# A hybrid decoder layer on one core: the head reordered so that x and the first weights are split first

## The chip, the cores and the metric

The kernel runs on one core of one Trainium2 chip. The metric is device time in microseconds (us), from the start to the end of one execution. Lower is better.

## The reference

One layer is computed for 520 tokens: 512 of a prompt and 8 of a sample group. Only its first part matters here.

```python
xn = rmsnorm(x, g1)               # x * rsqrt(mean(x*x) + EPS) * g1
z = xn @ w_in                     # q, k, v, o, ig, fg, u, vb, ga, gb
ig = ig + b_ig
lf = log_sigmoid(fg + b_fg)
h = mlstm_branch(q, k, v, ig, lf, ...)
u = gelu(u)
vn = rmsnorm(gelu(vb), g_v)
y_b = spatial_gate(u, vn, w_s, b_s) @ w_b
```

Behind it come the branch projections, an output projection, a second norm and a causal ConvFFN with D_FF 2816. All is in float32.

## The kernel before, in words

Tensors lie feature-major: 128 features on the partitions, 520 tokens in the row, and 1024 features are eight pieces (KT). Float32 products are made from two float32r halves. A value is split into `hi`, its rounded copy (ScalarE, function `split` for weights), and `lo`, the rest (VectorE, function `low`). One output tile of 128 features takes a weight slot of 128x1024 and 48 matmuls of 260 columns: for each of the eight pieces hi\*hi, hi\*lo and lo\*hi, over two halves of the tokens (function `tile`, L1293). Slots are numbered: 0 is the gate tile (gate rows ig and fg), 1 to 8 are the eight tiles of the v branch (vb 0 to 7), 9 to 12 the q tiles, and so on through some 150 slots. Raw weights, `whi`, `wlo` and the PSUM banks `out` are each double-buffered by the slot's parity. The counter `done` rises by one with each finished tile, and slot n is split only when the tile of slot n-2 is done.

A row norm commutes with a matmul. So the gate tile and vb 0 and 1 are computed on x times its gain without the norm (`xuh`, `xul`), and their results are multiplied by the norm's factor `rbc1` afterwards. The other vb tiles and all later ones use the normed `xh`, `xl`, which cost a product on GpSimd (L1170, in place in x), a copy on ScalarE and a subtraction on VectorE (L784) for each piece.

The head, on each engine, in the written order:

- Sync issues the x chunks 0, 1 and 3 (each two pieces of x), then the weights of slots 0 and 1; ScalarE issues gains, x chunk 2 and the gate bias.
- ScalarE squares the even pieces of x, VectorE the odd ones, into two buffers `sq`. TensorE sums each square over the partitions by a matmul with ones into `aux` (32 float32 matmul instructions), and a buffer is written again only when TensorE has read it. Between the squares both engines split x; the weights of slot 0 are split before the last pair of pieces.
- ScalarE takes the root, VectorE the reciprocal (L775), and GpSimd then scales x, eight products.
- The v branch's result goes through a gelu on ScalarE into `ftmp`, is transposed on TensorE (L1322, in the middle of the next tile), copied to `g_tok` on VectorE (L842), and squared and summed on GpSimd (L1183, L1185). For vb 0 and 1 VectorE first scales the result (L789); for vb 2 to 7 gelu reads PSUM itself and so empties the bank.
- Between them VectorE does three blocks of small work on the gate rows: `gate_cumsums` (L803 to L811), `gate_maxima` (L816 to L823) and `gate_outputs` (L828 to L836), behind vb 3, 4 and 5. ScalarE makes the softplus (absolute value, exp, log, each with a table load) around vb 2 and 3.

Every engine runs its own list in order, so what stands ahead in a list is what delays the next item. Nothing behind the q tiles is touched by the change.

Of the kernel before, what the change touches and what calls it, by code (L numbers as in the profile page):

```python
# [75 lines left out]
def hybrid_layer(nc, ins, outs):  # L76
    with ExitStack() as ctx:
# [332 lines left out]
        def _(act):  # L410
# [67 lines left out]
            split(At(2))  # L478
            for k in range(4):
                normed_hi(k)  # L480
            split(At(3))
            for k in range(4, 6):
                normed_hi(k)
            scaled_vb(0)
            for k in range(6, KT):
                normed_hi(k)
            split(At(4))
            scaled_vb(1)


            def vb_step(i, t):
                n = At(S_VB + t, i, 2)
                split(n.plus(2))
                apart()
                ready(n)
                act.wait_ge(tr_done, n(-2))
                A(gvs[:, i * 2 + t, :], smp(n), ACT.Gelu_apprx_tanh)
                A(both(ftmp[t][:, :]), out2(n), ACT.Gelu_apprx_tanh).then_inc(evac[n.c % 2], 1)


            vb_step(1, 0)
            evacuated(act, At(S_GATE))
            act.wait_ge(s_const, 16)
            A(lfe[:, :], fg[:, :], ACT.Abs, bias=gb[:, 1:2])
            act.drain()
            A(lfe[:, :], lfe[:, :], ACT.Exp, scale=-1.0)
            vb_step(1, 1)
            act.drain()
            A(lfe[:, :], lfe[:, :], ACT.Ln, bias=ones[0:NH, 0:1]).then_inc(s_ln, 1)
            with act.Fori(2, 4) as i:  # L510
                for t in range(2):
                    vb_step(i, t)
# [222 lines left out]
        def _(dve):  # L735
# [26 lines left out]
            for r in range(KT // 2):  # L762
                dve.wait_ge(s_x[r], 16)
                if r >= 1:
                    dve.wait_ge(s_ssk, 2 * r)
                TT(sq[1][:, :], x0[:, 2 * r + 1, :], x0[:, 2 * r + 1, :], ALU.mult).then_inc(s_sq[1], 1)
                if r == KT // 2 - 1:
                    low(At(0))
                for k in (2 * r, 2 * r + 1):
                    dve.wait_ge(s_xuh, k + 1)  # L770
                    STT(xul[:, k, :], x0[:, k, :], gains[:, 0, k:k + 1], xuh[:, k, :].bitcast(F32),
                        ALU.mult, ALU.subtract).then_inc(s_xu, 1)
            low(At(1))
# [3 lines left out]
            ready(At(S_GATE))  # L777
            for at0, rows_ in ((0, ig), (32, fg)):
                o = TT(both(rows_[:, :]), out_ps[0][at0:at0 + NH, :, 0:HALF], both(rbc1[at0:at0 + NH, :]), ALU.mult)
            o.then_inc(evac[0], 1)  # L780
# [63 lines left out]
            def vb_step(j):  # L844

                n = At(S_VB + j)
                vb_side(j - 1)
                if 4 <= j <= 6:
                    (gate_cumsums, gate_maxima, gate_outputs)[j - 4]()
# [711 lines left out]
```

## Time and profile before

| | us |
|---|---|
| median of 3 runs | 933.81 (933.24 to 934.28) |
| the profiled execution | 933.54 |
| its span, first to last instruction | 931.2 |
| TensorE busy in matmuls | 907.6 (97%) |
| VectorE busy | 524.5 (56%) |
| ScalarE busy | 365.8 (39%) |
| GpSimd busy | 135.4 (15%) |

The profiled execution is 0.27 us below the median, and 2.3 us of it lie outside the span. TensorE is busy for 97% of the span, so the time is the sum of its work and of the few stretches in which it waits. These are at the two ends. The reader should go by where TensorE first starts real tiles, and by each gap in its row after that.

### The profile page before, as it was taken

Reading aid. Unit: us, or ns where it says so; the run is one execution under the profiler, and the core shown is the slowest. Engines: PE = TensorE matmul, PEld = TensorE weight load, DVE = VectorE, ACT = ScalarE, POOL = GpSimd, SP = SyncE. Lnnn points to the kernel's source line nnn. Section 1 sums busy time; section 2 is a strip of 40 time slices with the busy share of each in tenths; the row PEclk is TensorE's granted clock in tenths of the full one; section 3 lists DMA queues with packets and bytes.
Section 4 is the critical chain, followed back from the end, with each engine's and each line's share of the span. In section 5 each row is a group of like instructions: output and inputs, shape, how many; then the busy total and the mean of one; then the engine's idle time right before and its main releaser. Section 6 shows DMA issues by size and latency. Waiting matters only on the chain.

```text
span 931.2 us, 19618 instructions
## 1 busy us (share of the span) xinstructions
PE 907.6 (97%) x7424; PEld 899.8 (97%) x7424; DVE 524.5 (56%) x801; ACT 365.8 (39%) x550; POOL 135.4 (15%) x182
## 2 busy tenths in 40 slices
PE   7999999999999999999999999999999999999993
PEld 6999999999999999999999999999999999999993
DVE  7874555552784444433335777777777777332334
ACT  5663333543873223322223344444444444222230
POOL 1843000002451111000006600000000000000002
PEclk9999999999999999999999999999999999999997
DMA  5414233224782221342234222222222223323222
GB/s 183 124 66 151 92 113 128 79 70 161 256 287 91 89 68 68 117 156 90 90 106 103 90 91 90 90 90 90 90 90 92 91 92 99 97 83 103 83 62 92
DMA packets 30184, 100.16 MB, mean 108 GB/s; under 512 B 4524, under 2 KB 6604, under 8 KB 29896
## 3 DMA queue, kind: packets, MB, share of 16 engines
q1 hardware_dynamic: 28528, 93.46, 30.4%
q0 software_dynamic: 1328, 5.72, 2.3%
q8 instruction: 21, 0.34, 0.2%
q10 hardware_dynamic: 296, 0.55, 0.2%
q14 instruction: 11, 0.09, 0.0%
HBM read 92.37 MB, written 7.35 MB: 107 GB/s over the span
## 4 chain that ended last, share of the span: by engine, by line
PE 89%; DVE 4%; POOLq 3%; issue 2%; DMA 1%; POOL 0%; DVEq 0%; ACT 0%; ACTq 0%
PE out L1293 83%; PE aux L1293 2%; PE trp L1293 2%; POOLq L1270 2%; DVE xl L784 1%; POOLq L1268 1%; PE trp L1322 1%; DVE wlo L742 1%; DVE y L1154 1%; DMA gains<-in_gains 0%; PE aux L1427 0%; DVE ftmp L1150 0%; DMA cwb<-in_conv_wb 0%; DVE mmax L820 0%; POOL out_conv_old L1254 0%
## 5 line engine op out<-in xcount | busy, mean ns | idle before, releaser
L742 DVE TENSOR_TENSOR wlo<-raw,whi 128x1024 fp32r<-128x1024 f32 (+1 forms) x149 | 189.7, 1273 | 227.3 <-ACT whi L412 227.0
L412 ACT ACTIVATE whi<-raw 128x1024 fp32r<-128x1024 f32 (+1 forms) x149 | 156.3, 1049 | 266.0 <-PE out L1293 264.3
L1293 PE MATMUL out<-xh,whi 128*128 128x260 f32 x864 | 178.7, 288 | 1.2 <-DVE wlo L742 1.2
L1293 PE MATMUL out<-xh,wlo 128*128 128x260 f32 x864 | 173.9, 283 | 0.0
L1293 PE MATMUL out<-xl,whi 128*128 128x260 f32 x864 | 173.7, 282 | 0.0
L1293 PE MATMUL out<-x2h,wlo 128*128 128x260 f32 x704 | 141.9, 283 | 0.0
L1293 PE MATMUL out<-x2h,whi 128*128 128x260 f32 x704 | 141.8, 282 | 0.0
L1293 PE MATMUL out<-x2l,whi 128*128 128x260 f32 x704 | 141.6, 283 | 0.0
L1293 PEld LDWEIGHTS out<-xh,whi 128*128 128x128 f32 x864 | 133.4, 189 | 1.9 <-DVE wlo L742 1.4
L1293 PEld LDWEIGHTS out<-xh,wlo 128*128 128x128 f32 x864 | 133.1, 188 | 0.0
L1293 PEld LDWEIGHTS out<-xl,whi 128*128 128x128 f32 x864 | 133.0, 188 | 0.0
L1293 PEld LDWEIGHTS out<-x2h,whi 128*128 128x128 f32 x704 | 108.6, 188 | 0.1
L1293 PEld LDWEIGHTS out<-x2h,wlo 128*128 128x128 f32 x704 | 108.5, 188 | 0.0
L1293 PEld LDWEIGHTS out<-x2l,whi 128*128 128x128 f32 x704 | 108.2, 188 | 0.0
L1293 PE MATMUL out<-acth,wlo 128*128 128x260 f32 x352 | 71.0, 283 | 0.0
L1293 PE MATMUL out<-acth,whi 128*128 128x260 f32 x352 | 70.8, 282 | 0.0
L1293 PE MATMUL out<-actl,whi 128*128 128x260 f32 x352 | 70.8, 283 | 0.0
L1097 DVE TENSOR_TENSOR up<-out,rbc 128x520 f32<-128x520 f32 x44 | 30.9, 702 | 42.3 <-PE out L1293 42.2
L1293 PEld LDWEIGHTS out<-acth,wlo 128*128 128x128 f32 x352 | 54.3, 188 | 0.0
L1293 PEld LDWEIGHTS out<-acth,whi 128*128 128x128 f32 x352 | 54.2, 188 | 0.0
L1293 PEld LDWEIGHTS out<-actl,whi 128*128 128x128 f32 x352 | 54.1, 188 | 0.0
L1276 POOL COPY nconv<-up 128x10 f32 x44 | 9.0, 204 | 242.8 <-DVEq L1098 242.8
(254 smaller groups left out, 1269.5 us busy)
## 6 DMA issues: line engine op xcount, KB each, us to landing
raw<-in_w_slots SPq DMA_DIRECT2D x125, 512.0 KB, 3.3
raw<-in_w_dn SPq DMA_DIRECT2D x16, 448.0 KB, 3.3
c_ring<-in_C_state SPq DMA_DIRECT2D x8, 512.0 KB, 4.9
row<-scratch SPq DMA_DIRECT2D x8, 512.0 KB, 5.6
out_C_sample<-c_ring SPq DMA_DIRECT2D x8, 512.0 KB, 3.8
raw<-in_w_dn SPq DMA_DIRECT2D x8, 512.0 KB, 3.5
xres<-in_x_all POOLq DMA_DIRECT2D x1, 2080.0 KB, 11.2
x<-in_x_all SPq DMA_DIRECT2D x3, 520.0 KB, 5.7
```

The costliest lines, as they stand in the source:

```text
L412: return act.activation(out, in_, func, **kw_)
L742: TT(wlo[p][:, 0:width], raw[p][:, 0:width], whi[p][:, 0:width].bitcast(F32), ALU.subtract)\
L784: STT(xl[:, k, :], x0[:, k, :], gains[:, 0, k:k + 1], xh[:, k, :].bitcast(F32), ALU.mult, ALU.subtract).then_inc(s_xn, 1)
L1097: TT(both(up[t][:, 2:2 + TOK]), out2(n), both(rbc2[:, :]), ALU.mult).then_inc(evac[n.c % 2], 1)
L1154: TT(y[:, j, h], xg[:, j, h], rbcf[:, h], ALU.mult).then_inc(s_y, 1)
L1268: pool.drain()
L1270: pool.drain()
L1276: pool.tensor_copy(nconv[:, i * 2 + t, :], up[t][:, SEQ:2 + TOK]).then_inc(s_nc, 1)
L1293: return pe.matmul(*a, **k)
L1322: m = pe.transpose(trp[b.c % 2][:, c, :], ftmp[b.c % 2][:, c * P:(c + 1) * P], ident[:, :])
```

## The change

It does five things.

1. x and the first weights come first. Sync issues x chunk 0, weights 0, x chunk 3, weights 1; ScalarE issues gains, x chunks 1 and 2. ScalarE splits x piece 0, then the gate weights, then the other pieces, then the weights of slot 1; VectorE follows in the same order. No square stands between.
2. The squares move behind, all eight on ScalarE into `xsq`. VectorE adds them into `xsum` (seven additions), and one sum product on TensorE (two matmuls, four instructions) stands in the middle of vb 1, behind its first piece.
3. The gate tile's raw result is copied by ScalarE out of PSUM into `graw`, and VectorE scales it from there after vb 0 and 1.
4. All eight vb tiles use `xuh`, `xul`. So each result is first scaled by VectorE (function `scaled_vb`), which also empties the bank, and gelu (function `vb_gelu`) follows on ScalarE in `ftmp`. The normed x is first read by the q tiles; its pieces are made by ScalarE and VectorE in steps 2 to 6 (`XN_AT`).
5. The gate blocks stand one step later than before (behind vb 4, 5 and 6 by name), and the softplus stands in one piece in ScalarE's step 3.

```diff
+XN_AT = ((), (), (0,), (1, 2), (3, 4), (5, 6), (7,), ())
...
             wp = ins["w_slots"]
-            for k in (0, 1, 3):
+            for n, k in ((0, 0), (1, 3)):
                 sp.dma_start(x0[:, 2 * k:2 * k + 2, :], ins["x_all"][:, 2 * k:2 * k + 2, :]).then_inc(s_x[k], 16)
-            for n in range(2):
                 load(At(n), wp[n])
...
             act.dma_start(gains[:, :, :], ins["gains"]).then_inc(s_g, 16)
-            act.dma_start(x0[:, 4:6, :], ins["x_all"][:, 4:6, :]).then_inc(s_x[2], 16)
+            for k in (1, 2):
+                act.dma_start(x0[:, 2 * k:2 * k + 2, :], ins["x_all"][:, 2 * k:2 * k + 2, :]).then_inc(s_x[k], 16)
             act.dma_start(gb[:, :], ins["gate_b"]).then_inc(s_const, 16)
...
-                if k % 2 == 0:
-                    if k >= 2:
-                        act.wait_ge(s_ssk, k - 1)
-                    A(sq[0][:, :], x0[:, k, :], ACT.Square).then_inc(s_sq[0], 1)
-                if k == KT - 2:
-                    split(At(0))
                 A(xuh[:, k, :], x0[:, k, :], scale=gains[:, 0, k:k + 1]).then_inc(s_xuh, 1)
-            split(At(1))
-            act.wait_ge(done, 1)
+                if k == 0:
+                    split(At(S_GATE))
+            split(At(S_VB))
+
+            for k in range(KT):
+                if k == 4:
+                    split(At(S_VB + 1))
+                A(xsq[:, k, :], x0[:, k, :], ACT.Square).then_inc(s_sq, 1)
+            ready(At(S_GATE))
+            A(graw[:, :].rearrange("p (a b) -> p a b", a=2), out_ps[0][0:32 + NH, :, 0:HALF]).then_inc(evac[0], 1)
+            split(At(S_VB + 2))
+            act.wait_ge(s_ss1, 1)
...
+            def vb_gelu(j):
+
+                evacuated(act, At(S_VB + j))
+                A(gvs[:, j, :], ftmp[j % 2][:, SEQ:TOK], ACT.Gelu_apprx_tanh)
                 act.drain()
-                A(ftmp[j][:, :], ftmp[j][:, :], ACT.Gelu_apprx_tanh).then_inc(evac[(S_VB + j) % 2], 1)
...
+            for j in range(2, 8):
+
+                split(At(S_VB + j + 1))
+                if j == 2:
+                    vb_gelu(0)
+                vb_gelu(j - 1)
+                for k in XN_AT[j]:
+                    normed_hi(k)
+                if j == 3:
+                    act.wait_ge(s_gr, 1)
+                    act.wait_ge(s_const, 16)
+                    A(lfe[:, :], fg[:, :], ACT.Abs, bias=gb[:, 1:2])
+                    act.drain()
+                    A(lfe[:, :], lfe[:, :], ACT.Exp, scale=-1.0)
+                    act.drain()
+                    A(lfe[:, :], lfe[:, :], ACT.Ln, bias=ones[0:NH, 0:1]).then_inc(s_ln, 1)
+            split(At(S_VB + 9))
+            vb_gelu(7)
...
+            for k in range(KT):
+                dve.wait_ge(s_xuh, k + 1)
+                STT(xul[:, k, :], x0[:, k, :], gains[:, 0, k:k + 1], xuh[:, k, :].bitcast(F32),
+                    ALU.mult, ALU.subtract).then_inc(s_xu, 1)
+                if k == 0:
+                    low(At(S_GATE))
+            low(At(S_VB))
+            dve.wait_ge(s_sq, 2)
+            TT(xsum[:, :], xsq[:, 0, :], xsq[:, 1, :], ALU.add)
+            for k in range(2, KT):
+                if k == 5:
+                    low(At(S_VB + 1))
+                dve.wait_ge(s_sq, k + 1)
+                dve.drain()
+                m = TT(xsum[:, :], xsum[:, :], xsq[:, k, :], ALU.add)
+            m.then_inc(s_sum, 1)
+            low(At(S_VB + 2))
...
             def scaled_vb(j):
-                ready(At(S_VB + j))
-                TT(both(ftmp[j][:, :]), out2(At(S_VB + j)), both(rbc1[:, :]), ALU.mult).then_inc(s_raw, 1)
-
-            low(At(2))
-            for k in range(4):
-                normed_low(k)
+                n = At(S_VB + j)
+                ready(n)
+                if j >= 2:
+                    dve.wait_ge(tr_done, B_VB + j - 1)
+                TT(both(ftmp[j % 2][:, :]), out2(n), both(rbc1[:, :]), ALU.mult).then_inc(evac[n.c % 2], 1)
+
             scaled_vb(0)
-            low(At(3))
-            for k in range(4, KT):
-                normed_low(k)
             scaled_vb(1)
+            for at0, rows_ in ((0, ig), (32, fg)):
+                o = TT(rows_[:, :], graw[at0:at0 + NH, :], rbc1[at0:at0 + NH, :], ALU.mult)
+            o.then_inc(s_gr, 1)
 
...
-            for j in range(1, 8):
+                if j >= 3:
+                    scaled_vb(j - 1)
+                low(At(S_VB + j + 1))
+                if j == 3:
+                    vb_side(1)
+                for k in XN_AT[j]:
+                    normed_low(k)
+                if j >= 5:
+                    (gate_cumsums, gate_maxima, gate_outputs)[j - 5]()
+                vb_side(j - 1 if j >= 3 else 0)
+
+            for j in range(2, 8):
                 vb_step(j)
+            scaled_vb(7)
+            low(At(S_VB + 9))
             vb_side(7)
 
-            evacuated(dve, At(S_VB + 7))
+            dve.wait_ge(s_vbg, KT)
             TT(ssq[:, :, :], gvs[:, :, :], gvs[:, :, :], ALU.mult)
             dve.drain()
...
+            def transposes(b, evn, vb=None):
+
+                if vb is None:
+                    evacuated(pe, evn)
+                else:
+                    pe.wait_ge(s_vbg, vb + 1)
                 pe.wait_ge(tre[b.c % 2], b.half(1))
                 for c in range(NC):
...
+            def square_sums():
+
+                pe.wait_ge(s_sum, 1)
                 for a in range(2):
-                    m = MM(aux[:, a, 0:HALF], ones[:, :], sq[k % 2][:, a * HALF:(a + 1) * HALF],
-                           start=k == 0, stop=k == KT - 1)
...
+            def vb_transposes(j):
+
+                transposes(At(B_VB + j), None, vb=j)
 
             tile(At(S_GATE), xuh, xul, each=s_xu)
             tile(At(S_VB), xuh, xul)
+            tile(At(S_VB + 1), xuh, xul, mid_at=0, mid=square_sums)
             pe.wait_ge(s_tri, 1)
...
+            tile(At(S_VB + 2), xuh, xul, mid_at=4, mid=lambda: vb_transposes(0), end=lambda: vb_transposes(1))
+            for j in range(3, 8):
+                tile(At(S_VB + j), xuh, xul, mid_at=5, mid=lambda: vb_transposes(j - 1))
...
-            tile(At(S_Q), xh, xl, mid_at=5, mid=lambda: transposes(At(B_VB + 7), At(S_VB + 7)))
+            tile(At(S_Q), xh, xl, each=s_xn, mid_at=5, mid=lambda: vb_transposes(7))
```

ScalarE at the head of the program, before. `sq` are squares, `xuh` the high halves of x times gain, `whi` the high halves of weights, `rbc` the norm's factor.

```order
L412 ACTIVATE sq_119<-x_87 128x520
L412 ACTIVATE xuh<-x_87,gains 128x520 x2
L412 ACTIVATE sq_119<-x_87 128x520
L412 ACTIVATE xuh<-x_87,gains 128x520 x2
L412 ACTIVATE sq_119<-x_87 128x520
L412 ACTIVATE xuh<-x_87,gains 128x520 x2
L412 ACTIVATE sq_119<-x_87 128x520
L412 ACTIVATE whi_107<-raw_105 128x1024
L412 ACTIVATE xuh<-x_87,gains 128x520 x2
L412 ACTIVATE whi_108<-raw_106 128x1024
L412 ACTIVATE rbc_57<-aux,eps 128x520
```

The same place now:

```order
L417 ACTIVATE xuh<-x_89,gains 128x520
L417 ACTIVATE whi_110<-raw_108 128x1024
L417 ACTIVATE xuh<-x_89,gains 128x520 x7
L417 ACTIVATE whi_111<-raw_109 128x1024
L417 ACTIVATE xsq<-x_89 128x520 x4
L417 ACTIVATE whi_110<-raw_108 128x1024
L417 ACTIVATE xsq<-x_89 128x520 x4
L417 ACTIVATE graw<-out 36x520
L417 ACTIVATE whi_111<-raw_109 128x1024
L417 ACTIVATE rbc_59<-aux,eps 128x520
L417 ACTIVATE whi_110<-raw_108 128x1024
```

The squares (`xsq`) stood between the pieces of x and ahead of the gate weights; now the gate weights stand second, and the squares behind the weights of slot 1, four ahead of the weights of slot 2 and four behind.

VectorE in the middle of the v branch, before, from the split weights of slot 6 (`wlo`) to the next copy. `ig`, `lf` and `bcum` are the first gate block.

```order
L742 TENSOR_TENSOR wlo_109<-raw_105,whi_107 128x1024
L842 COPY g_tok<-trp 128x4x128
L803 TENSOR_SCALAR ig<-ig,gb 4x520
L805 TENSOR_SCALAR lf<-fg,gb 4x520
L807 TENSOR_TENSOR lf<-lf,lfe 4x520
L811 SCALAR_TENSOR_TENSOR bcum<-ones,lf 4x128 x4
L742 TENSOR_TENSOR wlo_110<-raw_106,whi_108 128x1024
L842 COPY g_tok<-trp 128x4x128
```

The same gate block now:

```order
L784 TENSOR_TENSOR ftmp_117<-out,rbc_59 128x520
L733 TENSOR_TENSOR wlo_113<-raw_109,whi_111 128x1024
L776 SCALAR_TENSOR_TENSOR xl<-x_89,gains,xh 128x520 x2
L795 TENSOR_SCALAR ig<-ig,gb 4x520
L797 TENSOR_SCALAR lf<-fg,gb 4x520
L799 TENSOR_TENSOR lf<-lf,lfe 4x520
L803 SCALAR_TENSOR_TENSOR bcum<-ones,lf 4x128 x4
L834 COPY g_tok<-trp 128x4x128
L784 TENSOR_TENSOR ftmp_118<-out,rbc_59 128x520
L733 TENSOR_TENSOR wlo_112<-raw_108,whi_110 128x1024
```

Before, gelu on ScalarE read PSUM and asked nothing of VectorE. Now the row `ftmp<-out`, on which gelu and with it the transposes wait, stands behind the whole gate block and the copy of `g_tok`, and two pieces of `xl` stand ahead of the block too.

VectorE one step on, before, from the end of the second gate block (`mmax`, `mrun`, `g`) into the third:

```order
L820 SCALAR_TENSOR_TENSOR mmax<-g_100,mrun 4x128
L822 TENSOR_TENSOR mrun<-bcum,mmax 4x1
L823 TENSOR_SCALAR g_100<-g_100,mmax 4x128
L742 TENSOR_TENSOR wlo_109<-raw_105,whi_107 128x1024
L842 COPY g_tok<-trp 128x4x128
L828 SCALAR_TENSOR_TENSOR g_100<-bcum,mmax 4x512
L829 TENSOR_SCALAR nmm<-mmax 4x512
```

Now:

```order
L812 SCALAR_TENSOR_TENSOR mmax<-g_102,mrun 4x128
L814 TENSOR_TENSOR mrun<-bcum,mmax 4x1
L815 TENSOR_SCALAR g_102<-g_102,mmax 4x128
L834 COPY g_tok<-trp 128x4x128
L784 TENSOR_TENSOR ftmp_117<-out,rbc_59 128x520
L733 TENSOR_TENSOR wlo_113<-raw_109,whi_111 128x1024
L820 SCALAR_TENSOR_TENSOR g_102<-bcum,mmax 4x512
```

The second gate block is now followed by the copy and by the scaled product of vb 6, and only then by the weights of slot 9.

## Rows read from the trace of the kernel before

**Rows 1.** Windows, TensorE's tiles: us, then busy time by engine, PEclk, DMA share, GB/s

```profile
33.40:74.30 40.90, 38.26 (x317) 37.83 (x318) 30.94 (x44) 23.73 (x33) 23.32 (x21) 1.00 0.34 105
...
74.30:912.00 837.70, 837.64 (x6910) 834.21 (x6909) 455.86 (x713) 321.00 (x487) 93.78 (x141) 1.00 0.33 106
```

**Rows 2.** Timeline, TensorE: start, us, operation, count, idle before and its releaser

```profile
15.78 0.51 PE L1293 MATMUL out<-xuh,whi 128*128 128x260 f32 x2
...
34.73 0.66 PE L1322 MATMUL trp<-ident,ftmp 128*128 128x128 f32 x4 [1.40 <-ACT ftmp L412]
...
46.10 0.60 PE L1322 MATMUL trp<-ident,ftmp 128*128 128x128 f32 x4
...
67.94 0.51 PE L1293 MATMUL out<-xh,whi 128*128 128x260 f32 x2 [1.18 <-DVE wlo L742]
...
78.59 0.60 PE L1322 MATMUL trp<-ident,ftmp 128*128 128x128 f32 x4
```

**Rows 3.** Windows of the matmuls into aux alone, columns as in rows 1

```profile
5.75:10.40 4.65, 4.65 (x11) 3.69 (x12) 0.00 (x0) 0.00 (x0) 1.00 0.98 400
...
10.40:15.78 5.38, 5.34 (x23) 3.51 (x21) 0.00 (x0) 0.00 (x0) 1.00 0.00 2
```

**Rows 4.** DMA queue q1 in 0 to 6.1 and 0 to 9.1: packets, MB, share

```profile
q1 hardware_dynamic: 275, 1.06, 50.9%
...
q1 hardware_dynamic: 584, 2.18, 64.3%
```

**Rows 5.** DMA issues in 0 to 9.1: count, KB each, us to landing

```profile
raw<-in_w_slots SPq DMA_DIRECT2D x2, 512.0 KB, 7.9
```

**Rows 6.** Timeline, ScalarE and VectorE, 4 to 19 us

```profile
4.97 0.64 ACT L412 ACTIVATE sq<-x 128x520 f32<-128x520 f32 x1 [1.10 <-DMA gains<-in_gains]
...
10.28 1.43 DVE L771 SCALAR_TENSOR_TENSOR xul<-x,gains,xuh 128x520 fp32r<-128x520 f32 x2
...
13.42 1.04 ACT L412 ACTIVATE whi<-raw 128x1024 fp32r<-128x1024 f32 x1
...
14.50 1.23 DVE L742 TENSOR_TENSOR wlo<-raw,whi 128x1024 fp32r<-128x1024 f32 x1
...
18.12 3.40 DVE L775 RECIPROCAL rbc<-rbc 128x520 f32<-128x520 f32 x1
```

**Rows 7.** Timeline, VectorE and GpSimd, 21 to 65 us

```profile
21.67 13.99 POOL L1170 TENSOR_TENSOR x<-x,rbc 128x520 f32<-128x520 f32 x8 [19.21 <-DVE rbc L775]
...
25.26 6.98 DVE L784 SCALAR_TENSOR_TENSOR xl<-x,gains,xh 128x520 fp32r<-128x520 f32 x4
...
32.27 0.70 DVE L789 TENSOR_TENSOR ftmp<-out,rbc 128x520 f32<-128x520 f32 x1
...
41.04 1.04 POOL L1183 TENSOR_TENSOR sqt<-g_tok 128x512 f32 x1
...
61.89 1.28 POOL L1185 TENSOR_TENSOR acct<-acct,sqt 128x512 f32<-128x512 f32 x1
...
62.09 1.09 DVE L822 TENSOR_TENSOR mrun<-bcum,mmax 4x1 f32<-4x1 f32 x1
...
64.09 0.15 DVE L822 TENSOR_TENSOR mrun<-bcum,mmax 4x1 f32<-4x1 f32 x1
```

**Rows 8.** Timeline, VectorE, the ends of the first two gate blocks

```profile
53.55 0.47 DVE L803 TENSOR_SCALAR ig<-ig,gb 4x520 f32<-4x520 f32 x1
...
58.27 1.19 DVE L742 TENSOR_TENSOR wlo<-raw,whi 128x1024 fp32r<-128x1024 f32 x1
...
60.16 0.68 DVE L816 TENSOR_TENSOR g<-ig,bcum 4x512 f32<-4x512 f32 x1
...
66.66 1.23 DVE L742 TENSOR_TENSOR wlo<-raw,whi 128x1024 fp32r<-128x1024 f32 x1
```

**Rows 9.** Timeline, ScalarE, 34 to 46 us

```profile
34.04 0.64 ACT L412 ACTIVATE ftmp<-ftmp 128x520 f32<-128x520 f32 x1
...
44.31 1.28 ACT L412 ACT_TABLE_LOAD   x1
```

More of the change, by code:

```diff
@@ L99, in hybrid_layer @@
         xg = at("xg", [P, KT, TOK], 0)
+        xsum = at("xsum", [P, TOK], 0)
+        xsq = at("xsq", [P, KT, TOK], XB)
         y = at("y", [P, KT, TOK], XB)
@@ L245, in hybrid_layer @@
         s_tri = sem("triangles_made")
-        s_sq = [sem("even_square_ready"), sem("odd_square_ready")]
+        s_sq = sem("squares_ready")
+        s_sum = sem("square_sum_ready")
+        s_ss1 = sem("square_sum_broadcast")
+        s_gr = sem("gate_rows_scaled")
+        s_vbg = sem("vb_gelu_ready")
         s_xuh = sem("x_gain_hi")
@@ L478, in _ @@
-            split(At(2))
-            for k in range(4):
[L480 to L498, printed above, removed]
@@ L501, in _ @@
[L501 to L512, printed above, removed]
+                A(ftmp[j % 2][:, :], ftmp[j % 2][:, :], ACT.Gelu_apprx_tanh).then_inc(s_vbg, 1)
@@ L761, in _ @@
             dve.wait_ge(s_g, 16)
[L762 to L773, printed above, removed]
+            for k in range(KT):
[15 more added lines that the diff above has]
+            low(At(S_VB + 2))
             dve.wait_ge(s_std, 1)
@@ L776, in _ @@
             dve.drain()
[L777 to L780, printed above, removed]
             def normed_low(k):
@@ L844, in vb_step @@
             def vb_step(j):
[L846 to L849, printed above, removed]
-                low(n.plus(2))
-            for j in range(1, 8):
+                if j >= 3:
[9 more added lines that the diff above has]
+            for j in range(2, 8):
                 vb_step(j)
+            scaled_vb(7)
+            low(At(S_VB + 9))
             vb_side(7)
-            evacuated(dve, At(S_VB + 7))
+            dve.wait_ge(s_vbg, KT)
             TT(ssq[:, :, :], gvs[:, :, :], gvs[:, :, :], ALU.mult)
@@ L1323, in transposes @@
                 m.then_inc(tr_done, 1)
-            pe.wait_ge(evac[0], 1)
-            for k in range(KT):
-                pe.wait_ge(s_sq[k % 2], k // 2 + 1)
+            def square_sums():
+                pe.wait_ge(s_sum, 1)
                 for a in range(2):
-                    m = MM(aux[:, a, 0:HALF], ones[:, :], sq[k % 2][:, a * HALF:(a + 1) * HALF],
-                           start=k == 0, stop=k == KT - 1)
-                m.then_inc(s_ssk if k < KT - 1 else done, 1)
-            def vb_tile(i, t, each=None):
-                n = At(S_VB + t, i, 2)
-                tile(n, xh, xl, each=each, mid_at=5, mid=lambda: transposes(At(B_VB + t - 1, i, 2), n.plus(-1)))
+                    m = MM(aux[:, a, 0:HALF], ones[:, :], xsum[:, a * HALF:(a + 1) * HALF], start=True, stop=True)
+                m.then_inc(s_ss1, 1)
+            def vb_transposes(j):
+                transposes(At(B_VB + j), None, vb=j)
             tile(At(S_GATE), xuh, xul, each=s_xu)
             tile(At(S_VB), xuh, xul)
+            tile(At(S_VB + 1), xuh, xul, mid_at=0, mid=square_sums)
             pe.wait_ge(s_tri, 1)
-            tile(At(S_VB + 1), xuh, xul, end=lambda: transposes(At(B_VB), At(S_VB)))
-            vb_tile(1, 0, each=s_xn)
-            vb_tile(1, 1)
-            with pe.Fori(2, 4) as i:
-                for t in range(2):
-                    vb_tile(i, t)
+            tile(At(S_VB + 2), xuh, xul, mid_at=4, mid=lambda: vb_transposes(0), end=lambda: vb_transposes(1))
+            for j in range(3, 8):
+                tile(At(S_VB + j), xuh, xul, mid_at=5, mid=lambda: vb_transposes(j - 1))
             def v_sums():
```

13 lines of the change are left out of this document (3 added, 10 removed).

## The prediction

> **What bounds the kernel now.** I read the windows first, for the stretches in which TensorE waits. From 74.3 to 912 us it is busy for 837.64 of 837.70 us; there nothing but its own work counts, and the change touches nothing there. From 33.4 to 74.3 us it is busy for 38.26 of 40.90, so 2.6 us are lost [rows 1]. TensorE's own timeline says where: 1.40 us ahead of the first transposes, for a gelu on ScalarE, and 1.18 us at 67.94, for the low halves of a weight tile [rows 2]. The largest loss is ahead of all this: the first real tile starts at 15.78 [rows 2]. So the time is the start of the first tile, plus fixed work, plus gaps. The point to compare is the start of the first q tile, since nothing changes behind it. Its six first pieces end at 78.59, where the transposes stand. One v tile with its transposes takes (78.59-46.10-1.18 of gap)/5 = 6.26 us [rows 2], of which I take 0.45 for the transposes and 0.72 for each of eight pieces. So the q tile starts at 78.59 - 6 x 0.72 = 74.3.
>
> **Part 1: the head.** Removed is the chain of squares, buffers and sums. What is left ahead of the first tile is: x piece 0 split, gate weights landed, split high, split low. x and gains are there at 4.97 [rows 6]. In the weights' own queue the first 1.06 MB have passed by 6.1 us and 2.18 by 9.1 [rows 4]. Gate weights now stand second in it, so their last byte is number 1.05 million, at 6.1; before it was number 2.1 million. Two such loads land 7.9 us after issue [rows 5], about 10.1, some 0.8 behind their last byte. So they land at 6.9. ScalarE takes 1.04 and VectorE 1.23 [rows 6], so the gate tile starts at 9.3 instead of 15.78: 6.5 us won. VectorE then makes a low half of x every 0.67 us (two in 1.43, the next starting a little before the end) [rows 6], faster than a warm tile's 0.72, so it does not hold TensorE.
>
> Against that stands the clock. TensorE's first instructions, the sums into aux, came 11 in 4.65 us and then 23 in 5.38 with waits between them [rows 3]; each is 260 columns passed twice, so 0.42 us is the lower level of 1.2 GHz, though the clock column reads 1.00 in both. Before, those 4.65 us fell on sums that waited anyway. Now they fall on the gate tile and cost half of them, 2.3 us. The gate tile ends at 9.3 + 5.8 + 2.3 = 17.3, not 21.8, so 4.5 us are left. The Trainium skill, "TensorE: Matmul & The Clock Gate", section on what is actually happening, says that the idle array is throttled to half and that sustained activity releases it; the trace agrees, and by it nothing gets round the 2.3 us.
>
> **Part 2: the sum.** The squares follow the weights of slot 1 on ScalarE. The last four stand behind the weights of slot 2, which wait for the gate tile's end (17.5), so they come to 20.8. VectorE's seven additions, 0.7 each plus a drain, end at 23.4; TensorE asks for the sum after vb 1's first piece, at 23.8. No wait, but four instructions of 0.22 plus a gap, 1.0 us, on TensorE's path. Root to 25.7, reciprocal of 3.4 [rows 6] to 29.1, and the product of vb 0 to 29.7; vb 2, which needs its bank, starts at 29.8. That fits by 0.1 us. If the sum came 1 us late, 1 us would be lost. Gelu of vb 0 ends at 33.1 (weights of slot 4 to 31.1, a table load of 1.28, gelu in two parts, 0.9 together [rows 9]); TensorE asks at 33.4. So the 1.40 us gap goes. vb 3 starts at 36.4.
>
> **Part 3: the chain of VectorE.** This is where I expect the loss. Before, gelu of vb 2 to 7 read PSUM and asked nothing of VectorE. Now each transposition needs gelu, which needs VectorE's product, which stands behind that engine's whole previous step. TensorE asks for it 4.3 us into a tile; product and gelu take 1.7. So VectorE's previous step may overrun the start of the tile by 2.6 us, no more. And VectorE is slowed by GpSimd: while GpSimd scales x, an `xl` takes 6.98/4 = 1.75 us, against 0.72 for the like `xul` (1.43/2); a tiny `mrun` took 1.09 us, ending with GpSimd's addition at 63.18, against 0.15 with GpSimd idle; the scaled product, with one input in PSUM, keeps its 0.70 [rows 6, 7]. So I let a VectorE operation with two SBUF inputs, and the fast single-input forms, take turns with GpSimd's. The gate blocks took 4.7 us (53.55 to 58.27) and 6.5 (60.16 to 66.66), with about 1.6 of turns in each [rows 8].
>
> GpSimd's work moves too. It scaled x from 21.67 for 13.99 us [rows 7]; now it starts at 29.2, ends at 42.3, and its squares start 5.4 us later as before (35.66 to 41.04 [rows 7]), at 47.6, with three copies waiting, so it is busy without a break until about 60, under VectorE's steps 4 and 5. Working each list in order with these durations gives:
>
> - Step 3. ScalarE's softplus in one piece: high halves 1 and 2 of x end at 41.3, then three passes over 520 columns like gelu's 0.64 with two table loads of 1.28 between [rows 9], drains and all to 45.5, weights of slot 6 to 46.5, table and gelu of vb 3 to 48.5. vb 4 started at 42.6 and asks at 46.9. Gap 1.6.
> - Step 4 and 5. vb 5 starts at 50.4, vb 6 at 56.6. VectorE: xl 3 and 4 wait for ScalarE and take turns to 52.3, copy 52.9, product of vb 4 53.5, weights of slot 7 54.7, xl 5 and 6 with turns to 58.1, first gate block with turns to 62.9, copy 63.5, product of vb 5 64.2; gelu 65.1. TensorE asks at 56.6 + 4.3 = 60.9, and the wait for a semaphore adds a little. Gap 4.5, counting the rounding.
> - Step 6. vb 7 starts at 67.3. Weights of slot 8 to 65.8, xl 7 67.6, second gate block 4.9 without turns to 72.3, copy 72.9, product 73.5, gelu 74.4 and its wait. Asked for at 71.6. Gap 3.1.
> - Step 7: product of vb 7 78.9, gelu 79.9, asked for at 80.9. No gap.
>
> The q tile then starts at 76.6 instead of 74.3. As a test I reckoned the kernel before from its own lists in the same way: with turns its q tile starts at 73.8, without them at 70.7, where the trace has 74.3 [rows 2]. So turns belong in, and the reckoning is some 0.4 us short. The move of the gate rows out of PSUM costs a copy on ScalarE, like gelu's 0.64 [rows 9], hidden at 20.8 while it waits for a tile. The scaling of `ig` and `fg` from SBUF adds turns of 0 to 1.1 us each, since GpSimd scales x then; before no such row stands. I take 0.7 and 1.1. By the Trainium skill, "GPSIMD Engine Reference", section Key points, GpSimd shares its SBUF interfaces with VectorE where the latter has two SBUF inputs or a two-port mode; the trace agrees for `xl` and `mrun`, and the rule is what makes `ig` and `fg` dearer here.
>
> **The sum** at the first q tile: -6.5 start, +2.3 clock, +1.0 sum product, -2.6 old gaps and -1.1 small edges between the old tiles and rounding (the old stretch of 58.5 us holds 9 tiles, 7 sets of transposes and 2.6 of gaps, 57.6), +9.2 new gaps = +2.3. With the 0.3 that the reckoning falls short: +2.6. Made against the execution's 933.54 (0.27 below the median), that is 936.1 us.
>
> **Rivals.**
>
> 1. Turns miss. If GpSimd's squares fall where VectorE waits anyway, gaps 4.5 and 3.1 shrink. With none at all the same lists give one gap of 0.7, a q tile at 68.2, and 933.5 - 6.1 = 927.4. For it: turns depend on phase. Against: before could not be reckoned without them. This is the faster end; it decides when the product of vb 5 ends by 59.2. Chance 0.16 for 927.4 to 931.9.
> 2. Half the turns. Without those of the x scaling alone the lists give 73.8, so 933.54 - 0.5 = 933.0. For it: a turn is lost only where both engines ask at once, and `mrun` lost 0.9 once and nothing two microseconds later [rows 7]. Chance 0.28, within 0.2% (1.9 us, about what a measurement can tell from no change; 931.9 to 935.7).
> 3. The first weights don't come early. The x chunks in ScalarE's queue could be served ahead, and slot 0 land at 9.7 as before. The gate tile then starts at 12.1, 2.8 later, all later steps with it: q tile 79.5, 938.9. Against: queue q1 moved 1.06 MB by 6.1 with ScalarE's queue running beside it. Chance 0.07.
> 4. My forecast, chain and turns as reckoned, 934.8 to 937.8. Chance 0.49.
>
> **Numbers.** Predicted 936.1. The range is 930.0 to 938.6: below 930 lie most cases of rival 1, above it the late weights, together 0.15 to 0.2. By itself the forecast has 934.8 to 937.8. Part of the forecast and rival 3 lie above 935.7: slower 0.52; within 0.32; faster 0.16.
>
> **What would show it.** The first gate matmul at 9 to 10 us, 4 to 5 us of it at twice the later pitch; vb 2 at 29 to 31; in TensorE's timeline, gaps ahead of the transposes of vb 3, 5 and 6, released by ScalarE's `ftmp`, the largest that of vb 5, with VectorE busy without a break from 52 to 64. I am wrong if those gaps sum to under 6 us, if the gate tile starts after 11, or if a gap stands at a tile's start for its weights.

## The result and the profile after

The changed kernel takes 938.91 us (median of 4 runs, 936.54 to 939.21), the kernel before 933.52 beside it (4 runs, 932.38 to 934.28). The ratio is 1.0052, with an interval of 1.0040 to 1.0064: slower by about 4.9 us (the two medians lie 5.4 apart). Forecast were 936.1 and a range of 930.0 to 938.6, slower with a chance of 0.52. The direction is as forecast; the median is 2.8 above the figure. It is 0.3 above the range's end as it stands; by the ratio from the 933.54 on which the sum was made it is 938.4, inside it. The profiled execution took 936.54 us, 3.0 more than the one profiled before, with a span of 934.7 against 931.2. That it is the fastest of the four is part of the story below.

TensorE's timeline, the head and every stretch with a wait (start us, length us, what; in brackets the idle time before it and what ended it). These rows answer to [rows 2].

```profile
9.51 0.80 PE L1292 MATMUL out<-xuh,whi 128*128 128x260 f32 x2 [9.51 <-DVE wlo L733]
...
23.79 1.04 PE L1292 MATMUL aux<-xsum,ones 128*128 128x260 f32 x4
...
33.60 0.60 PE L1324 MATMUL trp<-ident,ftmp 128*128 128x128 f32 x4
...
49.30 0.65 PE L1324 MATMUL trp<-ident,ftmp 128*128 128x128 f32 x4 [1.96 <-ACT ftmp L417]
...
65.95 1.12 PE L1324 MATMUL trp<-ident,ftmp 128*128 128x128 f32 x4 [4.02 <-ACT ftmp L417]
...
75.78 0.66 PE L1324 MATMUL trp<-ident,ftmp 128*128 128x128 f32 x4 [0.74 <-ACT ftmp L417]
...
82.04 0.60 PE L1324 MATMUL trp<-ident,ftmp 128*128 128x128 f32 x4
```

The first real tile starts at 9.51 instead of 15.78. The sum product follows at 23.79 without a wait, and the transposes of vb 0 need none: the old gap of 1.40 is gone. Three new gaps stand ahead of the transposes of vb 3, 5 and 6, all released by gelu's `ftmp`. The last transposes start at 82.04 against 78.59 before; six pieces of 0.72 earlier, the first q tile starts at 77.7 against 74.3. So the v branch has given back all of the head and 3.4 us more, and these 3.4 are the difference of the spans (3.5) within rounding.

The windows of the gate tile (columns: stretch, its length, busy time and instructions of TensorE, weight load, VectorE, ScalarE, GpSimd, then TensorE's granted clock) answer to [rows 3].

```profile
9.50:14.00 4.50, 4.50 (x21) 4.50 (x22) 4.50 (x7) 4.18 (x7) 0.00 (x0) 1.00 0.52 200
14.00:17.50 3.50, 3.50 (x31) 3.50 (x31) 3.29 (x5) 2.02 (x4) 0.00 (x0) 1.00 0.26 81
```

In the first 4.5 us TensorE issues 4.7 matmuls per us (21 in 4.5), then 8.9 (31 in 3.5). The clock column shows 1.00 in both, as it did before; the pace of 260 columns each tells that the first stretch is at 1.2 GHz and the second at 2.4.

The same columns later, behind the gap of 4.02 us:

```profile
66.00:67.00 1.00, 1.00 (x5) 1.00 (x6) 0.53 (x2) 0.51 (x1) 0.98 (x1) 0.50 0.00 0
67.00:68.00 1.00, 1.00 (x7) 1.00 (x6) 0.91 (x2) 0.00 (x0) 0.87 (x1) 0.50 0.71 131
...
71.00:72.00 1.00, 1.00 (x7) 1.00 (x7) 0.84 (x4) 0.00 (x0) 0.00 (x0) 0.58 0.00 0
72.00:73.00 1.00, 1.00 (x11) 1.00 (x10) 0.86 (x3) 0.00 (x0) 0.00 (x0) 1.00 0.00 0
```

Here the granted clock itself reads 0.50, until just before 72. TensorE is busy without a break, but does half the work. The prediction has no such step.

VectorE's timeline, from the weights of slot 7 to the product of vb 6, answers to [rows 8].

```profile
52.88 0.68 DVE L784 TENSOR_TENSOR ftmp<-out,rbc 128x520 f32<-128x520 f32 x1
53.49 2.28 DVE L733 TENSOR_TENSOR wlo<-raw,whi 128x1024 fp32r<-128x1024 f32 x1
55.70 3.25 DVE L776 SCALAR_TENSOR_TENSOR xl<-x,gains,xh 128x520 fp32r<-128x520 f32 x2
58.87 1.26 DVE L795 TENSOR_SCALAR ig<-ig,gb 4x520 f32<-4x520 f32 x1
60.05 1.50 DVE L797 TENSOR_SCALAR lf<-fg,gb 4x520 f32<-4x520 f32 x1
...
63.69 0.65 DVE L834 COPY g_tok<-trp 128x512 f32<-128x512 f32 x1
64.27 0.68 DVE L784 TENSOR_TENSOR ftmp<-out,rbc 128x520 f32<-128x520 f32 x1
...
67.63 1.59 DVE L808 TENSOR_TENSOR g<-ig,bcum 4x512 f32<-4x512 f32 x1
...
74.09 0.69 DVE L784 TENSOR_TENSOR ftmp<-out,rbc 128x520 f32<-128x520 f32 x1
```

VectorE has hardly a pause from 49.9 to 64.9. The product of vb 5 (64.27) is the row that gelu and the 4.02 us gap wait for; since the product of vb 4 (52.88) all of slot 7's split, two pieces of `xl` and the gate block have stood ahead of it. GpSimd runs beside them; its timeline there:

```profile
58.64 1.21 POOL L1182 TENSOR_TENSOR sqt<-g_tok 128x512 f32 x1 [0.25 <-issue]
59.99 1.28 POOL L1184 TENSOR_TENSOR acct<-acct,sqt 128x512 f32<-128x512 f32 x1
```

`ig` ends at 60.1 and `lf` at 61.5, 0.3 behind the ends of GpSimd's rows at 59.85 and 61.27, and they take 1.3 and 1.5. The run without squares, below, has the same two rows with GpSimd idle: 0.47 each.

ScalarE's timeline around the softplus, where the gap of 1.96 comes from, answers to [rows 9]:

```profile
42.06 1.28 ACT L417 ACT_TABLE_LOAD   x1
...
44.05 1.28 ACT L417 ACT_TABLE_LOAD   x1
...
45.98 1.04 ACT L417 ACTIVATE whi<-raw 128x1024 fp32r<-128x1024 f32 x1
47.04 1.28 ACT L417 ACT_TABLE_LOAD   x1
48.33 0.21 ACT L417 ACTIVATE gvs<-ftmp 128x8 f32<-128x8 f32 x1
48.60 0.64 ACT L417 ACTIVATE ftmp<-ftmp 128x520 f32<-128x520 f32 x1
```

The product of vb 3 had been ready since 45.0. Gelu of vb 3 starts at 48.33, behind the softplus, a split of weights and a third table load; TensorE had asked at 47.34.

### The profile page after: what moved, and what is told of

The parts are those of the page before. It is cut to its first block, busy times and chain, and to the rows that moved or that the text cites. A ratio compares the mean times of both kernels' runs of the same rounds, so it can differ in the third digit from the quotient of the medians.

```text
span 934.7 us, 19551 instructions
## 1 busy us (share of the span) xinstructions
PE 903.3 (97%) x7396; PEld 897.9 (96%) x7396; DVE 531.4 (57%) x810; ACT 364.0 (39%) x551; POOL 137.3 (15%) x182
## 4 chain that ended last, share of the span: by engine, by line
PE 87%; DVE 4%; POOLq 3%; issue 2%; ACT 1%; DMA 1%; DVEq 1%; POOL 0%; ACTq 0%; SPq 0%
PE out L1292 82%; PE trp L1292 2%; POOLq L1269 2%; PE aux L1292 1%; POOLq L1267 1%; DVE xl L776 1%; PE trp L1324 1%; DMA raw<-in_w_slots 1%; DVE y L1153 1%; DVE wlo L733 0%; PE aux L1427 0%; DVE ftmp L1149 0%; DVE ftmp L784 0%; DMA cwb<-in_conv_wb 0%; ACT L417 0%
## 5 line engine op out<-in xcount | busy, mean ns | idle before, releaser
L1292 PE MATMUL out<-xh,whi 128*128 128x260 f32 x768 | 158.7, 288 | 0.0
L1292 PE MATMUL out<-xh,wlo 128*128 128x260 f32 x768 | 154.6, 283 | 0.0
L1292 PE MATMUL out<-xl,whi 128*128 128x260 f32 x768 | 154.3, 283 | 0.0
L1292 PEld LDWEIGHTS out<-xh,whi 128*128 128x128 f32 x768 | 118.7, 189 | 0.5
L1292 PEld LDWEIGHTS out<-xh,wlo 128*128 128x128 f32 x768 | 118.3, 188 | 0.0
L1292 PEld LDWEIGHTS out<-xl,whi 128*128 128x128 f32 x768 | 118.2, 188 | 0.0
```

The costliest lines, as they stand in the source:

```text
L1292: return pe.matmul(*a, **k)
```

## The experiments

My theory: the new gaps come from VectorE's and ScalarE's order (gate blocks and softplus ahead of what gelu needs), stretched by turns with GpSimd. Rival A: turns alone. Rival B: the clock, falling behind the gaps, takes a share of its own. Rival C: the head gains less than it seems. In each short diff, `-` and `+` are against the changed kernel unless the text says otherwise. Each time is a median, with its range; the kernel before took 933.43 beside the first four, 933.32 beside the next four and 933.14 beside the last.

**Again.** The changed kernel, unedited.

> The changed kernel once more, for its interval and a second profile. My theory (the gaps follow from VectorE's step order and GpSimd's turns, so they should repeat within some tenths): gaps of about 2.0, 4.0 and 0.7 us ahead of the transposes of vb 3, 5 and 6, one fall of TensorE's clock behind the second, span 934 to 938 us. Rival (the runs near 939 have something that the profiled run at 936.5 has not): in this profile a further gap, a longer stretch at the lower clock or a later first tile, worth 2 to 3 us together.

Measured: 938.87 us (936.14 to 939.16), ratio 1.0050 [1.0036, 1.0064]. The profiled execution this time took 938.34, near the median. Its TensorE timeline:

```profile
48.64 0.66 PE L1324 MATMUL trp<-ident,ftmp 128*128 128x128 f32 x4 [1.96 <-ACT ftmp L417]
...
56.41 0.60 PE L1324 MATMUL trp<-ident,ftmp 128*128 128x128 f32 x4
...
65.27 0.66 PE L1324 MATMUL trp<-ident,ftmp 128*128 128x128 f32 x4 [2.49 <-ACT ftmp L417]
...
75.12 1.12 PE L1324 MATMUL trp<-ident,ftmp 128*128 128x128 f32 x4 [3.42 <-ACT ftmp L417]
...
83.92 0.60 PE L1324 MATMUL trp<-ident,ftmp 128*128 128x128 f32 x4
```

and its windows:

```profile
50.50:51.50 1.00, 1.00 (x7) 1.00 (x6) 1.00 (x1) 0.18 (x1) 0.74 (x2) 0.50 0.05 12
...
77.00:79.00 2.00, 2.00 (x11) 2.00 (x11) 1.82 (x6) 0.07 (x1) 0.00 (x0) 0.50 0.71 258
```

The clock is at 0.50 twice, behind the first gap and behind the third. From a set of transposes that waited to the next set, a tile at the full clock takes 6.26 us (6.21 where nothing waited). Behind the first gap it took 56.41 - 48.64 = 7.77, so the fall cost 1.5; but the gap after it shrank from 4.02 to 2.49, by the same 1.5. Behind the third gap the step was 83.92 - 75.12 = 8.80, 2.5 more, and no gap follows that could take it up. In the first profile the fall stood behind the second gap: 75.78 - 65.95 - 0.74 = 9.09, so 2.8 more, and the third gap was 0.74 instead of the 3.42 here. So a fall of the clock is free while a later gap waits for VectorE anyway, and is paid where it comes behind the last one. That is the difference between the two profiled executions: the second stood 0.66 us ahead at the first gap (48.64 against 49.30) and 1.88 behind at the last transposes (83.92 against 82.04). That the other executions, seven of nine at 938.3 to 939.2 and two at 936.1 and 936.5, divide in the same way is inferred; they have no trace. I had expected one fall at the same place; there are two places, and they vary.

**Gate blocks late.** VectorE's three gate blocks stand in the first q tiles.

```diff
-                if j >= 5:
-                    (gate_cumsums, gate_maxima, gate_outputs)[j - 5]()
...
             low(At(S_Q + 2))
+            gate_cumsums()
...
             dve.reciprocal(rv[:, :], rv[:, :])
+            gate_maxima()
             low(At(S_Q + 4))
+            gate_outputs()
```

> The three blocks of gate work on VectorE moved out of steps 5 to 7 into the q tiles; nothing else. My theory (the gate blocks stand between a step and the product that gelu waits for): gaps ahead of the transposes of vb 5 and 6 vanish, the one of vb 3 stays (1.6 to 2.0), no fall of the clock, q tile at 69 to 70.5 us, time 929 to 931, that is 7 to 9 us below the changed kernel. Rival A (GpSimd's turns alone make the gaps): half of the gain at most, 934 to 936. Rival B (the work only moves and delays the q tiles' weights): gaps appear in the q tiles and the time stays within 2 us of the changed kernel.

Measured: 929.36 us (928.89 to 930.27), ratio 0.9952 [0.9939, 0.9966]: 9.5 less than the changed kernel. TensorE's timeline:

```profile
48.86 0.66 PE L1325 MATMUL trp<-ident,ftmp 128*128 128x128 f32 x4 [1.96 <-ACT ftmp L417]
...
56.63 0.60 PE L1325 MATMUL trp<-ident,ftmp 128*128 128x128 f32 x4
```

The gaps of vb 5 and 6 are gone, the softplus gap stays. The step from 48.86 to 56.63, 7.77, holds a fall, now behind the last gap and so paid. I had expected none. This profiled execution is also the slowest of the five (930.27); the others, at 928.9 to 929.5, would fit without the fall, but have no trace.

**No squares.** GpSimd's squares of the v rows and their sums are left out, so the factor made from them is made from zeros.

```diff
-                pool.tensor_tensor(sqt[:, :, :], g, g, ALU.mult)
-                pool.drain()
-                pool.tensor_tensor(acct[:, :, :], acct[:, :, :], sqt[:, :, :], ALU.add)
-                pool.drain()
...
+            pool.nop().then_inc(s_vss, 1)
```

The squares and sums of vb 6 and 7, which stand behind the loop, go too.

> GpSimd's squares and sums of the v rows are left out (the v norm's sums are then zero), so that GpSimd is idle after scaling x. My theory (turns with GpSimd are part of the chain): gap ahead of the transposes of vb 5 gone or under 0.5 us, of vb 6 about 1, of vb 3 unchanged, no fall of the clock, q tile near 70.5, time 6 to 8 us below the changed kernel. Rival (the gate blocks are too long whoever runs beside them): the gap of vb 5 stays over 2.5 us and the gain is under 3 us.

Measured: 930.62 us (930.0 to 931.21), ratio 0.9967 [0.9955, 0.9979]: 8.3 less. TensorE's timeline:

```profile
49.12 0.66 PE L1314 MATMUL trp<-ident,ftmp 128*128 128x128 f32 x4 [1.95 <-ACT ftmp L417]
...
61.59 0.60 PE L1314 MATMUL trp<-ident,ftmp 128*128 128x128 f32 x4
...
69.27 0.65 PE L1314 MATMUL trp<-ident,ftmp 128*128 128x128 f32 x4 [1.31 <-ACT ftmp L417]
```

and the first row of the gate block on VectorE:

```profile
55.31 0.47 DVE L795 TENSOR_SCALAR ig<-ig,gb 4x520 f32<-4x520 f32 x1
```

The gap of vb 5 is gone and that of vb 6 is 1.31. With the gate blocks where they stand, what is lost to GpSimd is thus the whole 4.0 and some 2 of the third, and the falls of the clock behind them; without the blocks the turns cost nothing (the run above). The two together make the gaps, so rival A falls as a cause by itself. The Trainium skill, "GPSIMD Engine Reference", section Key points, says that GpSimd's SBUF interfaces are shared with VectorE where the latter has two SBUF inputs or a two-port mode. The trace agrees in kind, and gives the size: the 4x520 rows `ig<-ig,gb` and `lf<-fg,gb` take 0.47 alone and 1.26 and 1.50 beside GpSimd, and a row with two inputs takes 0.69 alone (`lf<-lf,lfe`), where `ig` and `fg` from `graw` take 1.75 and 1.71 beside it. They hold almost no data, so this is about what waiting for one whole instruction of GpSimd's would give (its eight scalings of x take 14.07 us, 1.76 each).

**Warm.** 24 small products of ones into `aux`, ahead of the gate tile.

```diff
+            pe.wait_ge(evac[0], 1)
+            for _ in range(24):
+                MM(aux[:, 0, 0:P], ones[:, :], ones[:, :], start=True, stop=True)
```

> 24 small float32 products of ones into aux on TensorE ahead of the gate tile, so that it is busy from about 1.5 us; the result is not used. Theory of the cold start (the gate tile pays 2.3 us of half rate): first gate tile at 9.5 us and in 6 us instead of 8, vb 0 at 15.3 to 15.5 instead of 17.4, and all later steps 2 us earlier, time 2 us below the changed kernel, with the gaps of vb 3, 5 and 6 as they are. Rival A (the chain of VectorE absorbs an earlier start): same time within 0.5 us, gaps larger by 2 us in sum. Rival B: the small products run over 9.5 us and cost what they win.

Measured: 936.31 us (934.62 to 937.47, 9 runs), ratio 1.0030 [1.0020, 1.0040]. TensorE's timeline:

```profile
9.62 0.51 PE L1292 MATMUL out<-xuh,whi 128*128 128x260 f32 x2 [0.75 <-DVE wlo L733]
...
22.05 1.04 PE L1292 MATMUL aux<-xsum,ones 128*128 128x260 f32 x4
```

The sum product stands 12.43 behind the start of the gate tile; in the changed kernel it is 23.79 - 9.51 = 14.28, so the cold start had cost 1.85 us there. It varies: in the other profiles with a cold start the same stretch takes from 13.73 (again) to 14.51 (filler), so it costs 1.3 to 2.1. The time is 2.6 less: 1.7 is the earlier start, and the rest is within what the falls behind the gaps make of it. The gaps stay, 1.95, 3.84 and 2.08 us.

**Filler.** 8, 17 and 13 such products ahead of the transposes of vb 3, 5 and 6, in what were the gaps.

```diff
+                for _ in range(dict([(3, 8), (5, 17), (6, 13)]).get(j, 0)):
+                    MM(aux[:, 0, 0:P], ones[:, :], ones[:, :], start=True, stop=True)
```

> Small float32 products of ones into aux on TensorE stand ahead of the transposes of vb 3, 5 and 6 (8, 17 and 13 of them, about 0.21 us each), so that it is busy in the three gaps; the result is not used. Theory of the clock (the gaps let it fall, and the falls make both the extra loss and the spread from 936 to 939 us): no stretch at 1.2 GHz between the head and the end, q tile at 76.5 to 77.3 us, time 935.5 to 936.7, all runs within 1 us, 2 to 3 us below the median of the changed kernel. Rival (falls cost nothing, since the next gap shrinks by as much): same median as the changed kernel, or above it by what the small products overrun.

Measured: 936.47 us (935.89 to 937.11), ratio 1.0036 [1.0022, 1.0051]. TensorE's timeline:

```profile
47.16 1.95 PE L1292 MATMUL aux<-ones 128*128 128x128 f32 x16
49.27 0.66 PE L1324 MATMUL trp<-ident,ftmp 128*128 128x128 f32 x4 [0.16 <-ACT ftmp L417]
...
61.74 3.96 PE L1292 MATMUL aux<-ones 128*128 128x128 f32 x34
65.92 0.66 PE L1324 MATMUL trp<-ident,ftmp 128*128 128x128 f32 x4 [0.22 <-ACT ftmp L417]
...
72.18 3.07 PE L1292 MATMUL aux<-ones 128*128 128x128 f32 x26
75.77 0.66 PE L1324 MATMUL trp<-ident,ftmp 128*128 128x128 f32 x4 [0.52 <-ACT ftmp L417]
...
82.03 0.60 PE L1324 MATMUL trp<-ident,ftmp 128*128 128x128 f32 x4
```

and its windows, the granted clock at 1.00:

```profile
46.00:66.00 20.00, 19.62 (x166) 19.24 (x166) 17.55 (x18) 9.56 (x16) 13.66 (x10) 1.00 0.30 95
66.00:82.00 16.00, 15.48 (x130) 15.29 (x131) 14.45 (x26) 4.30 (x7) 7.65 (x6) 1.00 0.20 67
```

This run separates the two causes. With the gaps filled the clock stays up (1.00 in both windows), and the transposes stand within 0.03 us of where they stood in the first profile of the changed kernel: the chain sets them. The median is 2.4 below the changed kernel's and the spread is 1.2 instead of 2.7 to 3.0: these 2.4 are the falls. Their size is less certain than their existence: the means lie 1.8 to 1.9 apart, since two of the changed kernel's nine executions stand near 936 anyway, and the two ratios' intervals overlap. But all five executions here are at 937.11 or below, and seven of those nine at 938.34 or above. Filled and left time make the true gaps 2.1, 4.2 and 3.6.

**Old loads.** The loads issued as before: x chunk 1 with SyncE, ahead of the gate weights.

```diff
-            for n, k in ((0, 0), (1, 3)):
+            for k in (0, 1, 3):
...
+            for n in range(2):
...
-            for k in (1, 2):
+            for k in (2,):
```

> The loads issued as before (x chunks 0, 1, 3, then weights 0 and 1 on Sync; x chunk 2 on ScalarE), the rest as changed. Theory of the head (the gate tile starts two engine steps behind the landing of its weights, which is set by their place in the queue): gate weights land near 9.8 us, gate tile at 12.0 to 12.3 instead of 9.5, all later steps as much later, time 2 to 3 us above the changed kernel. Rival (the chain of VectorE sets the pace from vb 3 on, whatever the start): first tile later, but gaps smaller, time within 1 us.

Measured: 940.72 us (939.05 to 941.91), ratio 1.0077 [1.0063, 1.0091]. The gate tile starts at 12.07, 2.6 later, and the median is 1.9 longer (by the ratios about 2.4); the gaps are 2.28, 2.00 and 3.42. The delay passes through the gaps: the transposes of vb 5 stand at 67.96, 2.0 behind the first profile of the changed kernel and 2.7 behind the second. So the rival, that VectorE's chain sets the pace whatever the start, does not hold, and the order of the loads is worth about 2 us of its own.

**Softplus late too.** The gate blocks as above, and the softplus on ScalarE behind its first q step.

```diff
-                if j == 3:
-                    act.wait_ge(s_gr, 1)
...
+            q_step(0)
+            act.wait_ge(s_gr, 1)
+            act.wait_ge(s_const, 16)
+            A(lfe[:, :], fg[:, :], ACT.Abs, bias=gb[:, 1:2])
...
+            for j in range(1, NH):
```

> As with the gate blocks moved into the q tiles, and ScalarE's softplus moved behind the first q tile too. Theory (the gap of vb 3 is the softplus with its three table loads ahead of the split of slot 6): no gap over 0.3 us between the gate tile and the q tiles and no fall of the clock, q tile near 67.5 us, time 926 to 927.5, that is 2 to 3.5 us below the kernel with only the gate blocks moved. Rival (the softplus only moves the wait into the q tiles): a gap in the q tiles, time 928 to 930.

Measured: 927.45 us (926.82 to 928.09), ratio 0.9939 [0.9925, 0.9953]. No gap is left between the gate tile and the q tiles, and no fall. The window:

```profile
20.00:80.00 60.00, 59.95 (x499) 59.65 (x498) 45.55 (x44) 28.60 (x44) 40.56 (x30) 1.00 0.33 106
```

**Both, and warm.** The same with the 24 products ahead of the gate tile.

> The same with the 24 small products ahead of the gate tile. Theory: another 1.3 to 2 us, time 924.5 to 926; the sum product of the squares may wait 0.2 us, since the adds end just before it. Rival: the sum product and the bank of vb 0 become the bound, a gap of over 1 us stands in vb 1 or ahead of vb 2, and the gain is under 1 us.

Measured: 925.88 us (925.17 to 926.42), ratio 0.9923 [0.9909, 0.9937]. This is the best version, 7.4 below the kernel before and 13 below the changed one. The warm start is worth 1.6 here.

**Before, gate blocks late.** The kernel before, with its three gate blocks moved in the same way. The diff is against the kernel before.

```diff
-                if 4 <= j <= 6:
-                    (gate_cumsums, gate_maxima, gate_outputs)[j - 4]()
...
+            gate_cumsums()
...
+            gate_maxima()
...
+            gate_outputs()
```

> The kernel before with only the three gate blocks of VectorE moved into the q tiles. It asks how much of the fast versions' gain is the move alone. My theory (in the kernel before gelu does not wait for VectorE, so the blocks cost only the 1.18 us gap ahead of vb 7): that gap vanishes, the 1.40 us gap ahead of the first transposes stays, time 1.0 to 1.5 us below before, about 932. Rival (the blocks cost as much there as in the changed kernel): 5 us or more below before.

Measured: 931.67 us (931.13 to 932.59, 11 runs) against 933.14 (15 runs), ratio 0.9985 [0.9976, 0.9994]. TensorE's timeline:

```profile
34.23 0.65 PE L1323 MATMUL trp<-ident,ftmp 128*128 128x128 f32 x4 [1.40 <-ACT ftmp L412]
...
76.63 0.60 PE L1323 MATMUL trp<-ident,ftmp 128*128 128x128 f32 x4
```

The same move is worth 1.5 us before and 9.5 after. The blocks cost little where gelu asks nothing of VectorE, and much where it does. Between this kernel and the one with blocks and softplus late lie 931.67 - 927.45 = 4.2 us, which is what the new order is worth once nothing behind it takes it back. The old gap of 1.40, which this kernel still has, is part of it.

## Why the prediction was right, and where it fell short

**Part 1, the head: right.** The gate weights landed at 7.1 (the chain of waits, below; forecast 6.9) and the tile started at 9.51 (9.3). The loss to the low clock was 1.85 by the warm run and 1.3 to 2.1 over the profiles, forecast 2.3. That nothing gets round it was wrong: 24 small products ahead of the gate tile did. The old order of loads put the start at 12.07, which is rival 3's figure; it stood at 9.5, so rival 3 did not happen. Rival C falls too: the 4.2 us above are close to what the prediction gives (6.5 - 2.3 - 1.0 and the old gap of 1.40, 4.6).

```profile
1.28 5.84 DMA raw<-in_w_slots
7.14 1.06 ACT whi L417
8.23 1.24 DVE wlo L733
```

The chain goes from the load through both halves of the weights to the first row of TensorE at 9.51; x is not in it.

**Part 2, the sum product: right to 0.2.** It was forecast for 23.8 and taken at 23.79, four matmuls in 1.04 us, no wait. That it fits so well is partly luck: a start 0.2 late and a cold start 0.4 cheaper than reckoned cancel. The margin of 0.1 behind it did not hold: vb 2 starts at 29.94, 0.46 behind the row before it where the usual distance is 0.24, since the product of vb 0, which frees its bank, starts at 29.09 and takes 0.7.

**Part 3, the chain: right in place, order and size.** VectorE's products of vb 4 to 7 ended at 53.6, 65.0, 74.8 and 80.4; forecast were 53.5, 64.2, 73.5 and 78.9. The gaps were forecast at 1.6, 4.5 and 3.1, together 9.2. With the clock held up by filler they are 2.1, 4.2 and 3.6, together 9.9; in the first profile they are 6.7, because a slow tile filled most of the third. The `ig` and `fg` rows cost 1.75 and 1.71, at the dear end of what I allowed. The second gate block was reckoned without turns at 4.9; it took 5.8, since its first row (1.59) met GpSimd's addition, which ended at 68.68. No gap stood at step 7, as forecast.

**The turns: confirmed, but only together with the blocks.** Without the squares on GpSimd 8.3 us go, without the gate blocks 9.5. Rivals 1 and 2 let the turns miss, and they did not. What I wrote of them (the number of turns decides) holds only while the blocks stand in the chain.

**The sum: 1.1 short in the q tile.** It was forecast at 76.6 and starts at 77.7. Without any gap (gate blocks and softplus late) it starts at 67.8, where the forecast has 76.6 - 9.2 = 67.4; of these 0.4, some 0.2 are there when vb 2 starts (30.0, forecast 29.8). The rest is in the gaps: the profiled ones with the work that the slow tile did in place of the third (6.7 + 2.8 = 9.5), and 0.1 to 0.2 that each wait cost beside its gap, make 9.9 instead of 9.2. Two small terms of the sum do not follow from the numbers beside them: 58.5 - 57.6 is 0.9 and not 1.1, and the test on the kernel before falls short by 74.3 - 73.8 = 0.5 and not 0.3; with both the forecast is 936.5. From the last transposes to the end it takes 852.6 to 853.2 in every profile, so what is decided ahead of them reaches the end to within 0.6. Made against the profiled execution, the step gives 933.54 + 3.4 = 936.9, measured 936.54.

**The step that failed: the clock counted only at the head.** The prediction takes TensorE's fixed work as fixed once the head is past. The gaps that it forecast let the clock fall to half, and where that comes behind the last gap it costs 1.5 (the step of 7.77 with gate blocks late), 2.5 (8.80, again) or 2.7 (9.00, old loads). That is 2.4 us in the median, by the filler run, and it carried 936.5 to 938.9, past the range's end. The direction would have been the same without it. The Trainium skill, "TensorE: Matmul & The Clock Gate", section on HAM oscillation, warns of this: a kernel that waits within its matmul work is throttled again and starts its next work cold. The case in that section of the Trainium skill has waits for DMA of some 3 to 5 us. The traces agree for gaps of that size (3.42 to 4.02 us, each with a fall) and go beyond it: falls also stood behind some gaps of 1.96 to 2.28 us. I used that page of the Trainium skill for the head alone, though the forecast itself had three gaps in dense work. With the term in it, 936.1 + 2.4 is 938.5.

## What to carry to other kernels

A head start is worth what the next chain lets through: before counting it, follow each engine's list to the first operation that the bounding engine now asks of an engine that it did not ask before, and ask what stands ahead of it there. The cure was not in the head but in moving unrelated work (gate blocks, softplus) behind that operation; moving the gate blocks was worth six times more after the change than before it (9.5 us against 1.5). Where a forecast puts gaps into dense TensorE work, add what the slower clock costs behind the last of them, and no more than the next gap is long behind the others.

## What the runs showed of the hardware

- TensorE's granted clock fell to 0.50 at each of the four gaps of 3.42 to 4.02 us in the profiles (first, again, warm, old loads), at four of the nine between 1.95 and 2.49 us, and at none of the five between 0.74 and 1.40 us. In the first profile the gap of 1.96 was followed by a step of 55.56 - 49.30 = 6.26, at the full clock; in the second the same gap was followed by 7.77. What decides between them was not settled.
- The column of the granted clock reads 1.00 in the first microseconds of matmul work, in which a row of two matmuls takes 0.64 instead of 0.40 and starts 0.43 instead of 0.24 behind the one before; only later falls are shown in it. The pace of the rows has to be read there.
- VectorE rows of 4x520 with hardly any data took up to 1.75 us beside GpSimd, against 0.47 to 0.69 alone. The scaled product with one input in PSUM kept its 0.68 to 0.70 throughout.
- Three table loads of 1.28 us, 3.8 in all, stand in the 6.3 us between the first row of the softplus (`lfe<-fg,gb`, which ends at 42.0) and the start of gelu at 48.33: the softplus in one piece needs two, and gelu a third to come back. That is more than the gap of 1.96; that they alone make it was not tried.
